# The delta rule's triangular inverse: 16x16 diagonal blocks by substitution on GpSimd, and the first Gram product moved into the memory projection

## What is computed

```python
decay = jnp.exp(jnp.where(incl, g[..., :, None] - g[..., None, :], -jnp.inf))
kk = jnp.einsum('nbhid,nbhjd->nbhij', kc, kc)
lower = jnp.eye(c, dtype=F32) + jnp.where(strict, bc[..., :, None] * decay * kk, 0.0)
rhs = jnp.concatenate([bc[..., None] * vc, (bc * jnp.exp(g))[..., None] * kc], axis=-1)
sol = lax.linalg.triangular_solve(lower, rhs, left_side=True, lower=True, unit_diagonal=True)
qk = decay * jnp.einsum('nbhid,nbhjd->nbhij', qc, kc)
```

## Time and profile before

| | |
|---|---|
| median of 3 runs | 1666.29 us (1665.57 to 1668.97) |
| profiled execution, its own time | 1669.67 us |
| its span in the trace | 1668.0 us |
| TensorE busy | 1612.3 us, 97% |
| VectorE, ScalarE, GpSimd busy | 884.0, 537.4, 502.6 us |
| granted TensorE clock | 0.995 of full |

### The profile page before, as it was taken

How to read it: one execution, slowest core, us unless ns; L and a number is a source line. 1 busy time by engine, 2 the same in 40 slices (tenths; PEclk the granted TensorE clock), 3 DMA queues, 4 the chain that set the end, 5 groups by cost and what they waited for, 6 DMA issues and landing times. The chain is left out here.

```text
span 1668.0 us, 26092 instructions
## 1 busy us (share of the span) xinstructions
PE 1612.3 (97%) x10579; PEld 1541.0 (92%) x10579; DVE 884.0 (53%) x1288; ACT 537.4 (32%) x934; POOL 502.6 (30%) x379
## 2 busy tenths in 40 slices
PE   5999999999999999999999999999999999999999
PEld 4989989999999999998889899999999999889976
DVE  4667853344444442790387672435657552995611
ACT  6323243222222222233334443321145223664200
POOL 2333415333343411911244551222212121103400
PEclk9999999999999999999999999999999999999999
DMA  4211155223222114542366352235210341535521
GB/s 156 53 26 41 44 155 135 71 71 70 71 70 71 51 49 121 149 127 63 99 191 188 104 177 107 65 115 158 71 39 14 108 109 55 164 118 152 152 77 58
DMA packets 189365, 163.16 MB, mean 98 GB/s; under 512 B 18381, under 2 KB 157056, under 8 KB 188727
## 3 DMA queue, kind: packets, MB, share of 16 engines
q1 hardware_dynamic: 189246, 161.51, 33.4%
HBM read 131.38 MB, written 30.22 MB: 97 GB/s over the span
## 5 line engine op out<-in xcount | busy, mean ns | idle before, releaser
L276 POOL TENSOR_TENSOR wL<-w_raw,wH 128x1024 fp32r<-128x1024 f32 (+1 forms) x112 | 238.4, 2129 | 803.1 <-ACT wH L269 803.0
L335 PE MATMUL ps<-hH,wH 128*128 128x344 f32 x1920 | 458.2, 341 | 12.6 <-PEq L196 3.6
L335 PE MATMUL ps<-hL,wH 128*128 128x344 f32 x1920 | 420.1, 321 | 0.0
L335 PE MATMUL ps<-hH,wL 128*128 128x344 f32 x1920 | 419.4, 321 | 0.0
L335 PEld LDWEIGHTS ps<-hH,wH 128*128 128x128 f32 x1920 | 316.7, 190 | 26.5 <-issue 10.7
L335 PEld LDWEIGHTS ps<-hL,wH 128*128 128x128 f32 x1920 | 327.3, 189 | 0.2
L335 PEld LDWEIGHTS ps<-hH,wL 128*128 128x128 f32 x1920 | 324.9, 189 | 0.0
L269 ACT ACTIVATE wH<-w_raw 128x1024 fp32r<-128x1024 f32 (+1 forms) x116 | 108.5, 936 | 117.6 <-PE ps L335 107.2
L2918 POOL TENSOR_SCALAR fa_logits<-fox_c_bc,token_scalars 128x128 f32<-128x128 f32 (+7 forms) x32 | 58.7, 1834 | 51.9 <-DMA fox_c_bc<-rows_g_c_beta 27.0
L1880 ACT ACTIVATE d_m<-ps 128x512 f32<-128x512 f32 x48 | 28.7, 598 | 134.8 <-PE ps L2062 134.8
L1268 DVE SCALAR_TENSOR_TENSOR m_th<-m_th,ps 128x1032 f32<-128x1032 f32 x24 | 29.5, 1228 | 61.9 <-PE ps L335 61.9
(11 more groups left out here) (576 smaller groups left out, 2783.9 us busy)
## 6 DMA issues: line engine op xcount, KB each, us to landing
w_raw<-in_w_in SPq DMA_DIRECT2D x80, 512.0 KB, 5.1
m_th<-gate_spill SPq DMA_DIRECT2D x28, 516.0 KB, 4.5
gate_spill<-d_gate SPq DMA_DIRECT2D x18, 516.0 KB, 3.0
fa_kv<-in_cache_fox_k SPq DMA_DIRECT2D x32, 256.0 KB, 3.1
fa_kv<-in_cache_fox_v SPq DMA_DIRECT2D x32, 256.0 KB, 3.4
w_raw<-in_w_branch SPq DMA_DIRECT2D x32, 256.0 KB, 2.9
gate_spill<-fa_gate SPq DMA_DIRECT2D x10, 516.0 KB
x_rows<-in_x_prompt SPq DMA_DIRECT2D x8, 512.0 KB, 6.3
```

Of the source, the lines that this page charges most:

```text
L276: pool.tensor_tensor(self.wL[:, t % 2, 0:nk], self.raw_at(t)[:, 0:nk], self.wH[:, t % 2, 0:nk].bitcast(F32), ALU.subtract).then_inc(self.w ...
L335: last = pe.matmul(self.ps[:, b + g, 0:cols], w[:, t % 2, k], x[:, k, g * cols:(g + 1) * cols], start=(k == 0 and n == 0), stop=(k == nk - ...
```

## The change

- The inverse starts from blocks of 16 instead of 1. Once `NU` of a chunk is there, SP stores its eight 16x16 diagonal blocks of every head into a scratch tensor in DRAM, `d_blocks` (eight DMAs), and loads them back so that each of the 16 partitions of a block holds the whole block of each head (`NB_`, one DMA of 512 KB). GpSimd inverts all of them by substitution, one row of the inverse for each partition (`solve`: one copy and 15 pairs of a product and a sum), and spreads the 16 values over a 128x128 block-diagonal `Y` with a mask `BLK` (`spread`). TensorE turns `Y` into `X` (`turn`, now of `Y`, in slot 4 of the chunk itself), and VectorE copies it (`first_x`). Three levels (`LV = 3`) in slots 6 to 11 join blocks of 16, 32 and 64.
- GpSimd's preparation is cut in two, `decay` and `decayed_products`, with the low half of a weight tile between them, and `decay` waits for the norm of the chunk before the last.
- VectorE makes `NU` and `QKT` of the next chunk directly after `first_x`, ahead of the first level; before, after the third level.
- The first Gram product stands in the seventh tile of the memory projection, and its values are made at the end of VectorE's work there. The stage's other first pieces move by up to two steps of t0.
- Masks: two for `LO`, one for `UP` and one for `BLK` in place of fourteen. `NU` and `QKT` are allocated with the stage's outer tiles, `KS` has one buffer, and the squares share `M1`.

The diff, cut to its core:

```diff
-    LV = 6
+    LV = 3
     SLOTS = 16
+    NS = P // SB16
...
+        def gram_products(pe, ch):
+            for r in range(2):
+                for h in range(H):
+                    q = kT(ch, h) if r == 0 else qT(ch)[:, h]
+                    last = pe.matmul(B[6 + r][:, h], kT(ch, h), q, start=True, stop=True)
+            last.then_inc(S["gram"], 1)
+        def gram_values(dve, v, ch):
+            dve.wait_ge(S["qk"], ch + 1)
+            dve.wait_ge(S["gram"], ch + 1)
+            v.step(dve.tensor_tensor(NU[:, ch % 2], B[6], W[:], ALU.mult))
+            dve.tensor_tensor(QKT[:, ch % 2], B[7], DT[:], ALU.mult).then_inc(S["nu"], 1)
         class FirstChunk(Side):
-            def late_pe(self, pe, j, k): pass
+            def late_pe(self, pe, j, k):
+                if (j, k) == (6, 0):
+                    pe.wait_ge(units.tail.moved, 3)
+                    gram_products(pe, 0)
             def late_act(self, act, j):
                 if j == 5:
@@ -1759,7 +1792,9 @@
                     act.activation(DT[:], DT[:], ACT.Exp).then_inc(S["decay"], 1)
                     act.activation(GC[:, 0], GC[:, 0], ACT.Exp).then_inc(S["unit"], 1)
-            def late_dve(self, dve): pass
+            def late_dve(self, dve):
+                early(dve)
+                gram_values(dve, K.V(dve), 0)
...
+                def blocks(ch):
+                    sp.wait_ge(S["nu"], ch + 1)
+                    if ch:
+                        sp.wait_ge(S["block_in"], 16 * ch)
+                    for b in range(NS):
+                        part = slice(b * SB16, (b + 1) * SB16)
+                        sp.dma_start(K.d_blocks[b].rearrange("h m i -> m h i"), NU[part, ch % 2, :, part]
+                                     ).then_inc(S["block_out"], 16)
+                    sp.wait_ge(S["block_out"], 16 * NS * (ch + 1))
+                    if ch:
+                        sp.wait_ge(S["solved"], ch)
+                    else:
+                        before(sp)
+                    sp.dma_start(NB_[:].rearrange("p h m i -> p (h m i)"),
+                                 K.d_blocks.rearrange("b h m i -> b (h m i)").unsqueeze(1).broadcast_to(
+                                     [NS, SB16, H * SB16 * SB16])).then_inc(S["block_in"], 16)
+                blocks(0)
                 K.loads(sp, t0 + 3)
                 rows(1)
...
                     K.loads(sp, tile_of(ch, 0) + 3)
+                    if ch + 1 < NCH:
+                        blocks(ch + 1)
                     spill(tile_of(ch, 0))
                     K.loads(sp, tile_of(ch, 8) + 3)
...
+                def decay(ch):
                     pool.wait_ge(units.rows_in, 48 * (ch + 1))
                     if ch >= 1:
                         pool.wait_ge(S["nu"], ch)
+                    if ch >= 2:
+                        pool.wait_ge(S["on"], ch - 1)
                     g.do(pool.tensor_tensor(DT[:], GC[:, 0], bc(tokv(ch, 0)), ALU.subtract))
                     pool.tensor_tensor(DT[:], DT[:], mb(NEGM[:]), ALU.add).then_inc(S["diff"], 1)
-                    g.step(pool.tensor_tensor(W[:], GC[:, 2], mb(STR[:]), ALU.mult))
+                    g.do(pool.tensor_tensor(W[:], GC[:, 2], mb(STR[:]), ALU.mult))
+                def decayed_products(ch):
...
+                def solve(ch):
+                    pool.wait_ge(S["block_in"], 16 * (ch + 1))
+                    if ch == 0:
+                        pool.wait_ge(S["eye"], 1)
+                    g.do(pool.tensor_copy(YC[:], I16[:].unsqueeze(1).broadcast_to([P, H, SB16])))
+                    for m in range(SB16 - 1):
+                        n = SB16 - 1 - m
+                        term = pool.tensor_tensor(YT[:, :, 0:n], NB_[:, :, m, m + 1:SB16],
+                                                 YC[:, :, m:m + 1].broadcast_to([P, H, n]), ALU.mult)
+                        if m == SB16 - 2:
+                            term.then_inc(S["solved"], 1)
+                            pool.wait_ge(S["solved"], ch + 1)
+                        else:
+                            g.do(term)
+                        g.do(pool.tensor_tensor(YC[:, :, m + 1:SB16], YC[:, :, m + 1:SB16], YT[:, :, 0:n], ALU.add))
+                def spread(ch):
+                    if ch:
+                        pool.wait_ge(S["u"], ch)
+                    part = lambda x: x.rearrange("p (b i) -> p b i", i=SB16)
+                    pool.tensor_tensor(Y[:].rearrange("p h (b i) -> p h b i", i=SB16),
+                                      YC[:].unsqueeze(2).broadcast_to([P, H, NS, SB16]),
+                                      part(masks.BLK[:]).unsqueeze(1).broadcast_to([P, H, NS, SB16]), ALU.mult
+                                      ).then_inc(S["upy"], 1)
                 early(pool)
                 pool.memset(ST[:], 0.0).then_inc(S["zero"], 1)
-                identity(0)
-                prepare_gram(0)
+                decay(0)
+                decayed_products(0)
                 prepare_rows(0)
+                solve(0)
+                spread(0)
                 for ch in range(NCH):
                     if ch + 1 < NCH:
-                        prepare_gram(ch + 1)
+                        decay(ch + 1)
                     K.split_lo(pool, tile_of(ch, 0) + 2)
                     if ch + 1 < NCH:
+                        decayed_products(ch + 1)
                         prepare_rows(ch + 1)
                     K.split_lo(pool, tile_of(ch, 8) + 2)
                     if ch + 1 < NCH:
-                        identity(ch + 1)
+                        solve(ch + 1)
+                        spread(ch + 1)
                 K.split_lo(pool, END + 1)
...
-                        if s < 12 and s % 2 == 0:
-                            level(ch, s // 2 + 1)
-                        if s == 1 and ch + 1 < NCH:
-                            prepare_gram(ch + 1)
+                        if 6 <= s < 12 and s % 2 == 0:
+                            level(ch, s // 2 - 2)
                         if s in (2, 10):
                             K.split_hi(act, tile_of(ch, s) + 2)
+                        if s == 3 and ch + 1 < NCH:
+                            prepare_gram(ch + 1)
...
-                def first(ch):
+                def first_x(ch):
                     dve.wait_ge(S["turned"], ch + 1)
-                    dve.wait_ge(S["first"], ch + 1)
-                    dve.wait_ge(S["nu"], ch + 1)
-                    dve.copy_predicated(X[:], mb(LO[:, 0]), BM).then_inc(S["upx"], 1)
-                    dve.copy_predicated(Y[:], mb(UP[:, 0]), NU[:, ch % 2]).then_inc(S["upy"], 1)
+                    dve.tensor_copy(X[:], BM).then_inc(S["upx"], 1)
...
                 for ch in range(NCH):
                     if ch:
                         square_sums(ch - 1)
+                        norm(ch - 1)
+                    first_x(ch)
+                    if ch + 1 < NCH:
+                        gram_values(dve, v, ch + 1)
                     level(ch, 1)
-                    if ch:
-                        norm(ch - 1)
                     turned_x(ch, 2)
-                    level(ch, 2)
-                    turned_x(ch, 3)
-                    level(ch, 3)
-                    if ch + 1 < NCH:
-                        prepare_gram(ch + 1)
-                    turned_x(ch, 4)
-                    level(ch, 4)
                     if ch + 1 < NCH:
                         prepare_rows(ch + 1)
-                    turned_x(ch, 5)
-                    level(ch, 5)
+                    level(ch, 2)
                     decayed(ch)
-                    turned_x(ch, 6)
+                    turned_x(ch, 3)
                     rest(ch)
-                    level(ch, 6)
+                    level(ch, 3)
                     state(ch)
-                    if ch + 1 < NCH:
...
                 def turn(ch):
-                    pe.wait_ge(S["nu"], ch + 1)
+                    pe.wait_ge(S["upy"], ch * (LV + 1) + 1)
                     if ch:
                         pe.wait_ge(S["m1e"], ch * LV)
                     for h in range(H):
-                        last = pe.transpose(BM[:, h], NU[:, ch % 2, h], K.ident[:])
+                        last = pe.transpose(BM[:, h], Y[:, h], K.ident[:])
                     last.then_inc(S["turned"], 1)
...
                 for k in range(8):
                     bulk(t0, k)
-                    if k == 0:
-                        pe.wait_ge(units.tail.moved, 3)
+                    if k == 2:
+                        pe.wait_ge(S["nu"], 1)
                         pe.matmul(K.ps[:, 7, 0:NCH * H].rearrange("p (c h) -> p c h", h=H), masks.SEL[:],
                                   K.TK[:, :, 0], start=True, stop=True).then_inc(S["gl"], 1)
-                    if k == 2:
-                        pe.wait_ge(S["gld"], 1)
-                        pe.wait_ge(*K.emptied(t0 - 1))
-                        gram(0)
                     if k == 4:
                         rows(0)
-                    if k == 5:
```

(9 more changed lines are left out.)

## The result

The changed kernel takes 1661.71 us (median of 20 runs, 1654.91 to 1668.87), against 1666.39 us for the kernel before (20 runs beside them, 1663.03 to 1672.09). The ratio is 0.9973, interval 0.9963 to 0.9983: 4.7 us faster, where 25 had been forecast. The direction and the loop were as forecast, and the size was not. The rest of this text is on the missing 20 us, and on a version of the change that gets them and more.

A forecast was written before the change was run, and what follows sets the result against it. TensorE's queue was taken as the bound: 55.0 us saved, less 6.7 at the start and 22.8 for the new GpSimd and SP loop, gives 25.5, so 1666.29 becomes 1641 us. Range 1614 to 1670.

The forecast's parts named there:

- the loop: Delta stage, GpSimd and SP queue: from one chunk's decay to the next, forecast 41.5 us, longer than TensorE's 37.7.
- those 3.1 and the 5.0 of a weight tile behind a gate spill: Load back of blocks: bounded by 256 KB of rows alone (3.1 us) and a weight tile (5.0); 4.1 taken.
- the rival of few engines: Load back, 8 blocks outermost: eight DMA engines instead of sixteen, 1.7 us more a loop, 1651 us; chance 0.12.
- the two pieces ahead of the load: Decay to issue of the rows, forecast 12.8 us; issue of the rows to issue of the load back, 13.3.
- The 2.6 us of slot 8: Stage start: the product in slot 8 waits 2.6 us more, for X behind VectorE's Gram values.
- the 48.3: Whole kernel: gain in us left of TensorE's 55.0 after the start costs 6.7, before the loop's cost.
- the 22.8: Delta stage: loop's sixth spread 20.2 us later than TensorE would reach slot 4 of chunk 6, plus 2.6 of slot 8.
- lie beside TensorE and count nothing: VectorE's and ScalarE's saved copies and GpSimd's dropped masks: claimed to run beside TensorE, worth 0.
- the rival in which the loop fits: Delta stage: GpSimd and SP loop at or under 38.1 us, whole 48.3 us gained, 1618 us; chance 0.2.
- TensorE alone at 55.0: TensorE queue: 53.3 us from three fewer levels over eight chunks, plus 1.7 from moving the first Gram product.
- Each microsecond of P is worth six: Delta stage: P is the decay-to-decay length of the GpSimd and SP loop; each microsecond changes the kernel by six.
- At P = 45.8 nothing is left: Delta stage: break-even, where a decay-to-decay loop of 45.8 us eats the whole gain; forecast length 41.5.

The follow-up runs named there:

- the first experiment: Changed kernel with only SP's order changed: next chunk's blocks stored and loaded back before the rows of the chunk after are issued; 1625.47 us, ratio 0.9747.
- the second experiment: Changed kernel with each block stored twice, so the load back has 16 source blocks outermost instead of 8; 1670.05 us, ratio 1.0009.

## Why the forecast was off by 20 us

The bound and the prices. TensorE's queue set the time before, and a chunk without the three levels was put at 37.7 us. It is 37.3, as the first experiment's 38.0 less the gate wait of 0.73 shows: right within half a microsecond.

The loop. That the blocks queue behind the rows and the weight tile, that decay(N+2) comes a loop after decay(N+1), and that this loop exceeds TensorE's 37.7: right. With the rows out of it, or half of the solve, the waits for Y fell from 27.4 us to 3.6, all at the start, and to 1.0.

The failed step is a term of the sum: "The load back, 512 KB: between those 3.1 and the 5.0 of a weight tile behind a gate spill; 4.1 with a semaphore." It measured 7.2, outside of both of its bounds. The bounds were taken from transfers whose outermost dimension is 128; this one has 8. The prediction held such a mechanism, as the rival of few engines, but gave it 0.12 and priced it at 1.7 us a loop; by the second experiment the dimension is worth 2.5. The other 0.6 of the 3.1 I can't place: the spill and the weight tile issued right behind the load are there in that run too. Together with 0.5 more for the solve and 0.25 less for the two pieces ahead of the load (-0.4 and +0.15) the loop was 44.85 instead of 41.5, and six loops are 20.1 us.

A slip of the sum. The 2.6 us of slot 8 are taken off twice, once in the 48.3 and once in the 22.8. By its own terms the gain would have been 28.1 us and not 25.5.

The account is closed inside the stage, from its first bulk matmul to the product of the last chunk's values. Before, this took 632.00 - 275.47 = 356.5 us:

```profile
632.00 1.05 PE L2106 MATMUL ps<-d_vb,d_y 128*128 128x128 f32 x8
```

and in the changed kernel 626.34 - 271.68 = 354.7:

```profile
271.68 0.74 PE L336 MATMUL ps<-hH,wH 128*128 128x344 f32 x3 [1.16 <-POOL wL L277]
...
626.34 1.05 PE L2171 MATMUL ps<-d_vb,d_y 128*128 128x128 f32 x8
```

| piece | forecast | measured |
|---|---|---|
| begin to the first decay behind a spread | 22.43 | 294.60 - 271.68 = 22.92 |
| six loops | 249.0 | 269.11 |
| last decay of the loops to the turn | 0 | 0.10 |
| that turn to the next, the last | 37.7 | 42.29 |
| last turn to the values | 20.24, as measured | 626.34 - 606.10 = 20.24 |
| in all | 329.37 | 354.66 |

So the forecast's pieces are worth 27.1 us here, the change gave 1.9, and the missing 25.3 are the loops (20.1), the piece behind the last loop (4.6: the low clock 2.8, the Gram's wait 1.4, and 0.4 of the gate wait, which the shorter chunk leaves over; none of them in the sum), the start (0.5) and 0.1. The first experiment has 584.48 - 272.83 = 311.7, a gain of 44.9.

The other part of the 3.5 us between the profiled executions (1669.67 - 1666.15) lies outside the stage: the part ahead of it was 3.8 us shorter, and the part behind it 2.1 longer (1664.4 - 626.34 against 1668.0 - 632.00). What happened ahead can be read. TensorE's windows from 150 to 200 us, before and then changed:

```profile
150.00:200.00 50.00, 47.98 (x303) 47.68 (x304) 33.14 (x43) 16.39 (x20) 22.24 (x38) 0.97 0.14 36
150.00:200.00 50.00, 50.00 (x326) 49.71 (x326) 39.00 (x49) 16.42 (x20) 13.07 (x10) 1.00 0.14 33
```

In the kernel before TensorE waits 2.65 us until 152.02, behind a weight tile that came late, and the granted clock is then 0.63 from 152 to 154 and 0.52 from 154 to 156. In the changed kernel it doesn't wait there. Eight small stores stand ahead of that tile on SP and hold it for 10.1 us before and 7.3 in the changed kernel. Over all traces it is 10.1 and 9.8 in the two kernels with all the masks, and 7.2 to 7.9 in the six without. That the masks are the reason is not shown, but "lie beside TensorE and count nothing" can't be taken as right either. So of the 3.5 us between the two profiles only 1.9 come from the stage (1.7 of them by the Gram product, which now stands ahead of it), and how much of the 4.7 of the medians comes from outside the stage no run shows.

The new waits. The gate wait, nine times 0.73 us, was missed altogether. In the changed kernel most of it lies in the loop's shadow. In the first experiment it doesn't, and it is the largest reason why that one is at 1625 and not at the 1618 of the rival in which the loop fits: with TensorE alone at 55.0, the start's wait 3.6, 0.4 for X and 6.6 for the gate leave 44.4, where the stage gave 44.9. Two things left out of this nearly cancel: the first chunk's 2.2 us at the low clock, and chunks that are 0.4 us shorter each than priced. The wait in slot 8 at the start was put at 2.6 and measured 0.3; VectorE's values were earlier than I had them.

The clock. It fell, to 0.50, against the forecast. That cost 2.8 us once, and nothing in the loops. The forecast rested on the one gap of 1.7 us at this stage's start; the same trace has the gap of 2.65 us above, with a fall behind it.

The solve. 10.0 forecast, 10.6 measured in the mean; the small operations take 0.21 to 0.34 us with 0.07 between them. The fit from operations of 512 and 1024 elements was good down to 4 elements. The Trainium skill's "GPSIMD Engine Reference", section 3.1, from which I had estimated a fixed 0.31 us for each and a gain of about 5 us, gave the right total by the wrong term: an operation on 4 elements takes 0.21 in all, and the solve is far from the 13.4 of that estimate.

The sensitivity. "Each microsecond of P is worth six" held. "At P = 45.8 nothing is left" carries the slip of 2.6 us; without it the break-even is 46.2. The forecast stood 4.3 us from it by its own count, with a sum of several pieces, and that made it fragile. At 44.85 the rule gives (45.8 - 44.85) x 6 = 5.7 us, and the runs gave 4.7. That this is so near is luck in part: the 2.6 taken off twice stand in for the piece behind the last loop, which the sum didn't have.

## What to carry to other kernels

When work is taken off the engine that bounds a loop and put on a round trip through other engines and DRAM, write out the loop of the round trip, from one of its instructions to the same one an iteration later. What stands in it only by the order of a queue is the first thing to move: here the rows, issued ahead of the blocks, turned a gain of 42.5 us into one of 4.7, by an order on SP alone. A transfer is to be priced by one with the same outermost dimension and not by one with the same bytes. And a slot that is emptied stops hiding what it hid.

## What the runs showed of the hardware

- Behind waits of 4.8 and 4.1 us TensorE had a granted clock of 0.50 to 0.61 for some 3 to 7 us. In the kernel before it fell to 0.52 behind a wait of 2.65 us and stayed at 1.00 behind one of 1.71. Twelve small matmuls ahead of the wait kept it at 1.00 at a wait of 2.16 us and not at one of 2.12.
- 512 KB from DRAM took 7.2 us with eight blocks outermost, each read by 16 partitions, and 4.7 us with sixteen, each read by 8.
- Eight stores of 4 KB took 3.8 us of SP's time with nothing right ahead of them, and 8.8 us behind the rows and a weight tile: what stands ahead holds up the engine that issues, not only the transfers.
- A GpSimd operation on 4 elements for each partition took 0.21 us, on 60 elements mostly 0.29 to 0.34, and the gap between dependent ones was 0.07.
